# Three gates' units, their PSUM banks and four token sums placed differently in a two-block transformer kernel

## Chip, cores and metric

The kernel runs on one core of one Trainium2 chip (trn2). The metric is the time of one execution on the device in microseconds (us); lower is better. All data are float32. The engines are named as in the profile: PE is TensorE's matmul side and PEld its weight load, DVE is VectorE, ACT is ScalarE, POOL is GpSimd, and SP issues most of the transfers.

## The reference, cut to what matters

256 tokens of width 1024 go through two blocks one after the other. The first block is a token mixer (stick-breaking heads and dilated heads), a norm, 16 experts with two chosen for each token, and a norm. The second block is a mixer (retention of 4 heads beside a latent attention of 8 heads, each with a gate) and then 32 experts with four chosen for each token. The change lies in the two mixers.

```python
def merge_branches(ret_o, ret_gate, att_o, g_ret, g_mla, w_branch_ret, w_branch_mla, w_out):
    r = head_rms(ret_o).reshape(B, L, N_RET_HEADS * RET_V_DIM) * jax.nn.silu(ret_gate)
    m = att_o.reshape(B, L, N_MLA_HEADS * MLA_V_DIM)
    merged = jax.nn.sigmoid(g_ret) * (r @ w_branch_ret) + jax.nn.sigmoid(g_mla) * (m @ w_branch_mla)
    return merged @ w_out
...
    zl = split_proj(h_lat @ w_in)          # rq, rk, rv, rg, cq, ckv, kr, gr, gm
    ql, kl, vl = retention_qkv(zl[0], zl[1], zl[2], rope_fn)
```

## The kernel before

**Weights and phases.** SP streams weights in units of 2 MB into slots of a ring in SBUF, in the order of lists written out by hand: units of phase "a" (first mixer), the 16 experts, units of phase "b" (second mixer), the 32 experts. A unit is loaded as soon as the unit that held its slot has been multiplied, so TensorE's progress sets when transfers start. The number of bytes is the same in both kernels.

**PSUM banks.** There are eight banks. `open_tile` gives a tile the next bank in turn (of 8, or of the first 4 in the first mixer, `among=4`), or a named one, and TensorE waits until the tile that held the bank before has been read out and freed. TensorE executes its list in order, so a wait for one bank holds everything behind it.

**Seven products.** In the second mixer, 14 products of the 256 tokens with 1024 x 512 weights (the list `FAST`) are made by Strassen's scheme with seven products instead of eight, in `seven(i)`, and take three banks each (upper, Z, lower). VectorE makes four differences of each unit's weights (`sum_weights`, L2741) and combines the results (`combine(i)`, L2751 to L2762). ScalarE copies the first product aside (`first_copy(i)`, L2005). The left operands need four sums of the tokens' quarters: `sum_tokens` on VectorE (L2723 to L2726) makes them from the latent tokens once, and, for the unit `rv` of each retention head, from that head's turned tokens `uT`. A gate unit (`rg`: SiLU, `gr`: sigmoid) is read out by ScalarE in `gate_out(i)`, a unit `rq` is rotated by VectorE in `rope` (L2708 to L2714), 2 tiles of 512 columns each.

**Order on TensorE in the second mixer.** It runs seven(0), seven(1) (the two `rq` units), turns the latent tokens back into rows ("hl", L1225), turns the rotated keys and queries (`transposes("rkT", ...)`, `transposes("rqT", ...)`, L522), and runs seven(2). Then comes `scores(0)`, and for each head h of four: a gate's seven(2h+3), the head's turned tokens u (64 matmuls, L1319, with weights that VectorE makes in `weights(h)` from decays that ScalarE makes in `ret_decay(h)`), scores(h+1), and the values' seven(2h+4). Each tile of u is copied to `uT` by ScalarE (signal `uT_ready`). The values' products run in the order 1, 4, 2, 6, 5, 3, 7, and of these 6, 5, 3 and 7 wait for the token sums. A gate's run in the order 1, 6, 5, 2, 3, 7, 4.

**Banks there.** The turn stands at 14 when seven(0) starts, so seven(0) holds banks 6, 7, 0, seven(1) banks 1, 2, 3, the four "hl" tiles 4 to 7, and the four rkT tiles 0 to 3. The upper and lower tile of seven(1) are `rq` rows in banks 1 and 3, which VectorE frees after it has rotated them.

**Order in the first mixer.** TensorE multiplies the dilated values' first tile (`v_dl`, 0), the first two logits, the context's latent (`ckc`, two tiles) and the second tile (`v_dl`, 1). Then it goes through the dilated heads: for head h it turns the softmax's rows (`dl_turn`, L823), multiplies the values of head h-1, and does one other piece (a turn of conditioning rows `ada_turn`, L682, the turn of the context's latent, L760, the next logits). VectorE makes each head's maxima in `dl_max(h)` (L2310 to L2314), ScalarE the exponentials. Before dl_max(2) VectorE scales the stick-breaking heads (`head_norm`, L2326), reads out both ckc tiles and then copies (`v_dl`, 1).

**GpSimd** makes inverse roots on request (`root_of`, L1644), each a small power operation, and issues a few transfers.

## Time and profile before

| | |
|---|---|
| Time, median of 3 runs | 2136.42 us (2136.24 to 2136.6) |
| The profiled execution: own time | 2138.09 us |
| The profiled execution: span from first to last instruction | 2136.3 us |
| TensorE busy | 2059.3 us (96%) |
| VectorE busy | 658.2 us (31%) |
| ScalarE busy | 322.4 us (15%) |
| GpSimd busy | 45.3 us (2%) |
| Mean granted clock of TensorE | 0.992 |
| First mixer | about 10 to 205 us |
| 16 experts | about 205 to 669 us |
| Second mixer | about 669 to 1193 us |
| 32 experts | about 1193 to 2136 us |

The stages are read from the lines of the matmuls in TensorE's timeline. Busy time of a matmul group includes time in which the array runs at the lower clock, so it has to be read together with the granted clock of the stretch.

### The profile page before, as it was taken

Reading aid. Unit: us, or ns where it says so; the run is one execution under the profiler, and the core shown is the slowest. Engines: PE = TensorE matmul, PEld = TensorE weight load, DVE = VectorE, ACT = ScalarE, POOL = GpSimd, SP = SyncE. Lnnn points to the kernel's source line nnn. Section 1 sums busy time; section 2 is a strip of 40 time slices with the busy share of each in tenths; the row PEclk is TensorE's granted clock in tenths of the full one; section 3 lists DMA queues with packets and bytes.
Section 4 is the critical chain, followed back from the end, with each engine's and each line's share of the span. In section 5 each row is a group of like instructions: output and inputs, shape, how many; then the busy total and the mean of one; then the engine's idle time right before and its main releaser. Section 6 shows DMA issues by size and latency. Waiting matters only on the chain.

```text
span 2136.3 us, 23037 instructions
## 1 busy us (share of the span) xinstructions
PE 2059.3 (96%) x9259; PEld 968.1 (45%) x9262; DVE 658.2 (31%) x1286; ACT 322.4 (15%) x505; POOL 45.3 (2%) x66
## 2 busy tenths in 40 slices
PE   9999999989999899999999999999999999999997
PEld 6764333323334688887664433333333333333332
DVE  1665111101113844546551421222222212222213
ACT  1531111001002023212041100111111100111000
POOL 2011000000001000000000000000000000000000
PEclk9999999999999999999999999999999999999999
DMA  9975999999997422324525699999999999999996
GB/s 371 371 296 224 389 424 426 426 427 428 429 429 274 158 79 79 118 94 159 208 111 198 259 412 428 428 428 429 428 429 429 428 428 429 428 428 429 429 427 282
DMA packets 85904, 720.85 MB, mean 337 GB/s; under 512 B 6700, under 2 KB 12065, under 8 KB 46001
## 3 DMA queue, kind: packets, MB, share of 16 engines
q1 hardware_dynamic: 83744, 714.81, 81.0%
q0 software_dynamic: 2096, 5.16, 0.8%
q8 instruction: 44, 0.72, 0.2%
q14 instruction: 20, 0.16, 0.0%
HBM read 718.87 MB, written 1.08 MB: 337 GB/s over the span
## 4 chain that ended last, share of the span: by engine, by line
PE 70%; DMA 23%; DVE 5%; issue 1%; ACT 1%; POOL 0%; DVEq 0%; ACTq 0%; SPq 0%
PE bank L937 17%; PE bank L947 14%; DMA ring<-in_exp_w_gu 10%; DMA ring<-in_w_up 8%; PE bank L1285 6%; DMA pool<-in_exp_w_gu 5%; PE bank L575 4%; PE bank L545 3%; PE bank L954 3%; PE bank L917 3%; PE bank L640 3%; PE bank L1319 3%; PE bank L1376 2%; PE bank L929 2%; DVE ring L2741 1%
## 5 line engine op out<-in xcount | busy, mean ns | idle before, releaser
L937 PE MATMUL bank<-ring,pool 128*64 128x512 f32 x2176 | 485.5, 596 | 18.9 <-DMA ring<-in_w_up 14.9
L947 PE MATMUL bank<-ring,pool 128*64 128x512 f32 x1536 | 341.9, 595 | 9.6 <-DMA ring<-in_exp_w_gu 9.5
L937 PEld LDWEIGHTS bank<-ring,pool 128*64 128x64 f32 x2176 | 149.0, 137 | 310.1 <-issue 275.7
L947 PEld LDWEIGHTS bank<-ring,pool 128*64 128x64 f32 x1536 | 106.2, 137 | 220.0 <-issue 192.2
L1285 PE MATMUL bank<-ring,pool 128*128 128x256 f32 x784 | 172.2, 380 | 3.5 <-ACT ring L2005 1.9
L1285 PEld LDWEIGHTS bank<-ring,pool 128*128 128x128 f32 x784 | 148.5, 190 | 26.5 <-ACT ring L2005 3.1
L2605 DVE TENSOR_SCALAR pool<-bank 128x512 f32<-128x512 f32 x32 | 22.1, 691 | 408.7 <-PE bank L947 408.7
L1925 ACT ACTIVATE pool<-pool 128x512 f32<-128x512 f32 x32 | 20.1, 630 | 733.6 <-DVE pool L2605 733.6
L947 PE MATMUL bank<-pool 128*64 128x512 f32 x512 | 115.6, 594 | 6.4 <-DMA pool<-in_exp_w_gu 6.4
L1745 ACT ACTIVATE pool<-bank 128x512 f32<-128x512 f32 (+2 forms) x112 | 64.2, 573 | 272.9 <-PE bank L594 57.1
L2741 DVE TENSOR_TENSOR ring<-ring 128x1024 f32<-128x1024 f32 x72 | 88.2, 1225 | 34.5 <-issue 16.5
L954 PE MATMUL bank<-pool,junk 64*128 64x512 f32 x392 | 97.4, 615 | 1.5 <-DVE pool L2617 0.8
L917 PE MATMUL bank<-pool 128*64 128x512 f32 x384 | 94.6, 614 | 1.6 <-ACT pool L1745 1.6
L2602 DVE TENSOR_TENSOR pool<-pool,bank 128x512 f32<-128x512 f32 x16 | 17.0, 1059 | 230.1 <-PE bank L937 183.1
L937 PE MATMUL bank<-pool 128*64 128x512 f32 x384 | 86.6, 593 | 0.0
L575 PE MATMUL bank<-ring,pool 128*128 128x512 f32 x192 | 84.3, 594 | 1.4 <-ACTq L1748 1.4
L2617 DVE TENSOR_TENSOR pool<-bank,pool 128x512 f32<-128x512 f32 x32 | 22.1, 691 | 203.6 <-PE bank L937 203.6
L1915 ACT ACTIVATE pool<-bank 128x512 f32<-128x512 f32 x46 | 49.1, 1067 | 182.5 <-PE bank L917 182.5
L545 PE MATMUL bank<-ring,pool 128*128 128x512 f32 (+2 forms) x192 | 75.1, 549 | 1.3 <-DVEq L2296 1.3
L947 PEld LDWEIGHTS bank<-pool 128*64 128x64 f32 x512 | 36.1, 137 | 80.9 <-issue 69.2
L929 PE MATMUL bank<-pool,junk 32*64 32x512 f32 x256 | 61.8, 600 | 0.0
L1644 POOL TENSOR_TENSOR root<-root,power 128x1 f32<-128x1 f32 (+2 forms) x20 | 20.0, 999 | 1860.5 <-DVE root L2996 936.6
(436 smaller groups left out, 1813.9 us busy)
## 6 DMA issues: line engine op xcount, KB each, us to landing
ring<-in_exp_w_gu SPq DMA_DIRECT2D x96, 2048.0 KB, 25.4
ring<-in_exp_w_down SPq DMA_DIRECT2D x46, 2048.0 KB, 28.5
pool<-in_exp_w_gu SPq DMA_DIRECT2D x32, 2048.0 KB, 23.9
ring<-in_w_gate SPq DMA_DIRECT2D x30, 2048.0 KB, 23.1
ring<-in_w_up SPq DMA_DIRECT2D x30, 2048.0 KB, 25.0
ring<-in_w_down SPq DMA_DIRECT2D x30, 2048.0 KB, 21.9
ring<-in_w_in SPq DMA_DIRECT2D x21, 2048.0 KB, 8.2
pool<-in_exp_w_down SPq DMA_DIRECT2D x18, 2048.0 KB, 27.4
```

The costliest lines, as they stand in the source:

```text
L545: i = mm(ps[:, 0:width], src[:, k, t * P:(t + 1) * P], w[:, k, 0:width], start=(k == 0), stop=(k == w.shape[1] - 1))
L575: i = mm(banks[tiles[name, t, f][0]][:, :], srcT[:, kk, t * P:(t + 1) * P], w[:, k, f * 512:(f + 1) * 512], start=(kk == 0), stop=(kk == K ...
L640: i = mm(ps[:, m * T:(m + 1) * T], w[:, k, (2 * mp_ + m) * P:(2 * mp_ + m + 1) * P], xT[:, k, :], start=(k == 0), stop=(k == KC - 1))
L917: i = mm(XG[half[f], :], pick[:, t, :], src[:, t, f * 512:(f + 1) * 512], start=(t == 0), stop=(t == TC - 1))
L929: i = mm(dst[half[f], :], this_expert, bgu_rows[:, at:at + 512], start=True, stop=False)
L937: i = mm(dst[half[f], :], chunks[kk], rows[k][:, f * 512:(f + 1) * 512], start=(kk == 0), stop=(kk == KC - 1))
L947: i = mm(dst[half[f], :], chunks[2 * j + k], wide[:, k, at:at + 512], start=False, stop=(j == 3 and k == 1))
L954: i = mm(Y[t, f][:, :], put[half[f], t * P:(t + 1) * P], y_slot[half[f], :], start=False, stop=last, skip_group_check=True)
L1285: ins = mm(dst, left[:, k, :], right[:, k, :], start=(k == 0 and p != 2), stop=(k == 3), skip_group_check=True)
L1319: i = mm(ps[:, c * T:(c + 1) * T], in_rows[:, j, k * P:(k + 1) * P], dec2[:, j, :], start=(j == 0), stop=(j == 3))
L1745: freed(af(dst, view(ps), func, scale=scale), name)
L2741: mark(tt(to, x, y, ALU.subtract), "w_summed")
```

## The change

Five things change.

1. In `FAST`, the unit ("rg", 2) moves ahead of ("rv", 0). TensorE now runs seven(2) (the unit ("rg", 0)) between "hl" and the turns of keys and queries, with banks 2, 6, 7, and seven(3) after these turns, with banks 5, 6, 7. The turns get named banks: rkT 3, 4, 5, 6 and rqT 0, 1, 3, 4. The turn is rounded up to a multiple of 8 before seven(0) and before scores(0). Head 0's filler is seven(4) (("rg", 2)), head 1 has none, head 2's is seven(7), head 3's seven(9). The values' sevens are 5, 6, 8 and 10.
2. ScalarE reads out in the matching order: the four rkT tiles, gate_out(2), the four rqT tiles, first_copy(3), ret_decay(0), gate_out(3), first_copy(4). `first_copy(i)` also waits for the combined upper tile of i-1.
3. The four sums of each head's turned tokens are made by GpSimd, which waits for `uT_ready`, and for its own first sum, before it goes on. VectorE no longer makes them.
4. In the first mixer (`v_dl`, 0) goes to bank 4 and takes no turn of the four, the two ckc tiles swap banks 4 and 6, (`v_dl`, 1) is copied out by ScalarE instead of VectorE, and the context's latent is read out by VectorE behind dl_max(3) and turned by TensorE in head 3 instead of head 2.
5. Ahead of the first experts' placement, TensorE runs three warming matmuls (bf16, 512 columns) where it ran none.

```diff
-        FAST = (("rq", 0), ("rq", 1), ("rg", 0), ("rg", 1), ("rv", 0), ("rg", 2), ("rv", 1), ("rg", 3), ("rv", 2), ("gr", 0), ("rv", 3), ("gr", 1),
+        FAST = (("rq", 0), ("rq", 1), ("rg", 0), ("rg", 1), ("rg", 2), ("rv", 0), ("rv", 1), ("rg", 3), ("rv", 2), ("gr", 0), ("rv", 3), ("gr", 1),
                 ("gm", 0), ("gm", 1))
+        FILLER = {h: FAST.index(x) for h, x in ((0, ("rg", 2)), (2, ("rg", 3)), (3, ("gr", 0)))}
+        VALUE = [FAST.index(("rv", h)) for h in range(RH)]
...
-                ps = open_tile(pe, ("ckc", t), bank=(4, 6)[t])
+                ps = open_tile(pe, ("ckc", t), bank=(6, 4)[t])
...
-            by_rows([("v_dl", 0)], "a", n, part("a", n, KC, 512), [(xT, 0)], 512, among=4, last=False)
+            by_rows([("v_dl", 0)], "a", n, part("a", n, KC, 512), [(xT, 0)], 512, bank=4, last=False)
...
-                if h == 2:
+                if h == 3:
                     turn_context_latent()
...
-                keep_warm(ps, 0 if m == "m1" else 3)
+                keep_warm(ps, 3)
...
+            turn[0] += -turn[0] % 8
             for u in range(2):
                 seven(u)
             turn_back("hl", latT)
+            seven(2, (2, 6, 7))
             pe.wait_ge(S("rotated"), 4)
-            transposes("rkT", rk_rows, 4)
+            transposes("rkT", rk_rows, 4, at=(3, 4, 5, 6))
             pe.wait_ge(S("rotated"), 8)
-            transposes("rqT", rq_rows, 4)
-            seven(2)
+            transposes("rqT", rq_rows, 4, at=(0, 1, 3, 4))
+            seven(3, (5, 6, 7))
+            turn[0] += -turn[0] % 8
...
             for h in range(RH):
-                seven(2 * h + 3)
+                if h != 1:
+                    seven(FILLER[h])
...
-                seven(2 * h + 4)
+                seven(VALUE[h])
             seven(11)
...
-            inverse_roots(*([TC] * (RH + 2)))
+            for h in range(RH):
+                (x11, x12), (x21, x22) = token_quarters(uT)
+                s1, s2, s3, s4 = (u_sums[:, q] for q in range(4))
+                pool_eng.wait_ge(S("uT_ready"), 4 * h + 4)
+                if h > 0:
+                    pool_eng.wait_ge(S("product"), 7 * VALUE[h - 1] + 7)
+                nc.gpsimd.tensor_tensor(s1, x21, x22, ALU.add).then_inc(S("root_set"), 1)
+                pool_eng.wait_ge(S("root_set"), 2 * h + 6)
+                nc.gpsimd.tensor_tensor(s2, s1, x11, ALU.subtract).then_inc(S("root_set"), 1)
+                nc.gpsimd.tensor_tensor(s3, x11, x21, ALU.subtract)
+                pool_eng.wait_ge(S("root_set"), 2 * h + 7)
+                nc.gpsimd.tensor_tensor(s4, x12, s2, ALU.subtract).then_inc(S("tokens_summed"), 1)
+                inverse_roots(TC)
+            inverse_roots(TC, TC)
...
+                if h == 1:
+                    evac(v_dl[:, 1, :], ("v_dl", 1), lambda ps: ps[:, :], "v_ready")
...
             first_copy(2)
+            for cp in range(4):
+                evac(pairs(rkT[1], cp), ("rkT", cp), two, "rkT_ready", RQK ** -0.5)
+            gate_out(2)
+            for cp in range(4):
+                evac(pairs(rqT, cp), ("rqT", cp), two, "rows_and_rqT")
+            first_copy(3)
             ret_decay(0)
-            gate_out(2)
-            first_copy(3)
+            gate_out(3)
+            first_copy(4)
...
-            take_root(ckc_ss, 2 * HEADS, ckc_root)
-            for t in range(TC):
-                ps = tile(dve, ("ckc", t))
-                link(v.tensor_copy(krc[:, t, :], ps[:, KVR:CKR]))
-                mark(ts(ckn_c[:, t, :], ps[:, 0:KVR], ckc_ss[:, t:t + 1], None, ALU.mult), "ckc_ready")
-                freed(dve.nop(), ("ckc", t))
-            values_out("v_dl", v_dl, (1,))
+            def context_latent_out():
+                take_root(ckc_ss, 2 * HEADS, ckc_root)
+                for t in range(TC):
+                    ps = tile(dve, ("ckc", t))
...
 
             for h in range(2, HEADS):
                 dl_max(h)
+                if h == 3:
+                    context_latent_out()
...
             combine(2)
+            combine(3)
             weights(0)
             for h in range(RH):
-                combine(2 * h + 3)
-                dve.wait_ge(S("uT_ready"), 4 * h + 4)
-                sum_tokens(2 * h + 4)
+                if h != 1:
+                    combine(FILLER[h])
                 if h + 1 < RH:
                     weights(h + 1)
-                combine(2 * h + 4)
+                combine(VALUE[h])
```

## Rows read from the trace of the kernel before

**Rows 1.** The profile's page: busy time of the engines, and the chain that ended last
```profile
PE 2059.3 (96%) x9259; PEld 968.1 (45%) x9262; DVE 658.2 (31%) x1286; ACT 322.4 (15%) x505; POOL 45.3 (2%) x66
...
PE 70%; DMA 23%; DVE 5%; issue 1%; ACT 1%; POOL 0%; DVEq 0%; ACTq 0%; SPq 0%
```

**Rows 2.** What TensorE waited for: us in total, times, longest
```profile
PE bank L522 <- DVEq L2771: 7.3, 2, 6.0
...
PE bank L682 <- DVEq L2200: 2.9, 1, 2.9
```

**Rows 3.** TensorE's timeline: start, us, line, operation [idle before it, ended by]
```profile
739.51 1.91 PE L1225 MATMUL bank<-cst,pool 128*128 128x128 f32 x16
741.26 0.60 PE L522 MATMUL bank<-cst,ring 128*128 128x128 f32 x4
747.86 1.97 PE L522 MATMUL bank<-cst,ring 128*128 128x128 f32 x8 [6.00 <-DVEq L2771]
...
754.87 1.46 PE L1285 MATMUL bank<-ring,pool 128*128 128x256 f32 x6
```

**Rows 4.** Stretches: busy us of each engine, granted clock, DMA share, GB/s
```profile
137.00:143.00 6.00, 6.00 (x31) 5.27 (x30) 3.11 (x12) 3.20 (x11) 0.00 (x0) 0.50 1.01 414
744.00:755.00 11.00, 5.88 (x29) 5.48 (x30) 6.21 (x15) 3.32 (x6) 0.00 (x0) 0.53 0.26 100
...
1203.00:1204.00 1.00, 0.64 (x5) 0.58 (x6) 0.76 (x5) 0.00 (x0) 0.00 (x0) 1.00 0.00 0
```

**Rows 5.** TensorE's timeline, retention head 0
```profile
799.76 13.98 PE L1285 MATMUL bank<-ring,pool 128*128 128x256 f32 x64
814.02 3.72 PE L1285 MATMUL bank<-ring,pool 128*128 128x256 f32 x16 [0.28 <-DVE ring L2741]
818.37 7.17 PE L1285 MATMUL bank<-ring,pool 128*128 128x256 f32 x32 [0.62 <-ACT ring L2005]
```

**Rows 6.** TensorE's timeline, retention head 3
```profile
925.87 24.44 PE L1285 MATMUL bank<-ring,pool 128*128 128x256 f32 x112 [0.73 <-ACTq L1748]
```

**Rows 7.** VectorE's timeline, second mixer
```profile
736.74 0.42 DVE L2751 TENSOR_TENSOR ring<-ring,bank 128x256 f32<-128x256 f32 x1 [0.35 <-DVEq L2772]
...
743.01 0.42 DVE L2762 TENSOR_TENSOR bank<-bank,ring 128x256 f32<-128x256 f32 x1
...
750.55 0.42 DVE L2714 TENSOR_TENSOR pool<-pool 128x256 f32<-128x256 f32 x1
...
797.26 0.69 DVE L2723 TENSOR_TENSOR pool<-pool 128x512 f32<-128x512 f32 x1 [11.97 <-ACTq L1748]
...
807.17 0.69 DVE L2787 TENSOR_TENSOR pool<-pool 128x512 f32<-128x512 f32 x1 [7.16 <-ACT pool L1993]
```

**Rows 8.** ScalarE's timeline, second mixer
```profile
740.15 2.74 ACT L1745 ACTIVATE ring<-bank 128x512 f32<-128x512 f32 x4 [10.35 <-PE bank L1225]
...
757.20 1.28 ACT L1990 ACT_TABLE_LOAD   x1
```

**Rows 9.** GpSimd's timeline
```profile
186.24 0.55 POOL L1644 TENSOR_TENSOR root<-root,power 128x1 f32<-128x1 f32 x1 [19.20 <-DVE root L2173]
188.29 2.35 POOL L1696 TENSOR_TENSOR pool<-pool 128x1024 f32<-128x1024 f32 x1 [1.50 <-DVE pool L2433]
...
1173.15 0.53 POOL L1634 DMA_DIRECT2D pool<-in_exp_b_down  x1 [0.29 <-POOL pool L1718]
```

**Rows 10.** TensorE's timeline, first mixer
```profile
135.76 0.63 PE L682 MATMUL bank<-cst,misc 128*128 128x128 f32 x4 [2.92 <-DVEq L2200]
...
146.87 0.55 PE L823 MATMUL bank<-cst,pool 128*128 128x128 f32 x3
```

**Rows 11.** VectorE's timeline, first mixer
```profile
131.44 1.42 DVE L2326 TENSOR_TENSOR pool<-pool,stat 128x512 f32<-128x512 f32 x2
...
135.80 0.42 DVE L2310 TENSOR_TENSOR pool<-bank,pool 128x256 f32<-128x256 f32 x1 [0.24 <-DVE pool L2199]
...
138.38 0.16 DVE L2251 TENSOR_TENSOR mod<-bank,vecT 128x16 f32<-128x16 f32 x1
```

More of the change, by code:

```diff
@@ L537, in by_columns, with by_rows @@
                     multiplied(phase, n, (name, 1))
-            def by_rows(names, phase, n, w, srcs, width, among=8, last=True):
+            def by_rows(names, phase, n, w, srcs, width, among=8, last=True, bank=None):
                 landed(phase, n)
                 for name, (src, t) in zip(names, srcs):
-                    ps = open_tile(pe, name, among=among)
+                    ps = open_tile(pe, name, among=among, bank=bank)
                     for k in range(w.shape[1]):
@@ L1260, in _, with seven @@
             rk_rows_of(0, 1)
-            def seven(i):
+            def seven(i, at=(None, None, None)):
                 (first, second), sums = token_quarters(tokens_of(i)[0]), tokens_of(i)[1]
@@ L1267, in seven @@
                 landed("b", n)
-                Xb = open_tile(pe, upper)
-                Zb = open_tile(pe, ("seven", i))
-                Yb = open_tile(pe, lower)
+                Xb, Zb, Yb = (open_tile(pe, name, bank=b) for name, b in zip((upper, ("seven", i), lower), at))
                 sources = 2 + FAST[i][1] if FAST[i][0] == "rv" else 1
@@ L1718, in _ @@
             nc.gpsimd.memset(y_slot, 0.0).then_inc(S("root_set"), 1)
-            pool_eng.wait_ge(S("root_set"), 6)
+            pool_eng.wait_ge(S("root_set"), 14)
             for f in range(2):
@@ L2002, in first_copy @@
             def first_copy(i):
+                if i > 0:
+                    tile(act, row_tiles(i - 1)[0])
                 act.wait_ge(*after_product(i, 1))
@@ L2018, in _ @@
             first_copy(0)
-            tile(act, ("rq", 0, 0))
             first_copy(1)
             rows_back("hl", 2)
-            for cp in range(4):
-                evac(pairs(rkT[1], cp), ("rkT", cp), two, "rkT_ready", RQK ** -0.5)
-            for cp in range(4):
-                evac(pairs(rqT, cp), ("rqT", cp), two, "rows_and_rqT")
             def gate_out(i):
@@ L2035, in _ @@
             first_copy(2)
+            for cp in range(4):
[4 more added lines that the diff above has]
+            first_copy(3)
             ret_decay(0)
-            gate_out(2)
-            first_copy(3)
+            gate_out(3)
+            first_copy(4)
             rss = stat[:, 36:44]
             for h in range(RH):
-                gate_out(2 * h + 3)
+                if h != 1:
+                    gate_out(FILLER[h])
                 for g in range(4):
                     evac(pairs(uT, g), ("u", h, g), two, "uT_ready")
-                first_copy(2 * h + 4)
+                first_copy(VALUE[h])
                 if h + 1 < RH:
@@ L2050, in _ @@
                     act.wait_ge(S("ret_ss"), 2 * h + t + 1)
-                first_copy(2 * h + 5)
+                if h > 0:
+                    first_copy(VALUE[h] + 1)
             gate_out(11)
@@ L2065, in _ @@
             first_copy(12)
-            tile(act, ("gm", 0, 0))
             first_copy(13)
@@ L2362, in _ @@
             head_norm(0, "y_sb_ready")
-            take_root(ckc_ss, 2 * HEADS, ckc_root)
-            for t in range(TC):
-                ps = tile(dve, ("ckc", t))
-                link(v.tensor_copy(krc[:, t, :], ps[:, KVR:CKR]))
-                mark(ts(ckn_c[:, t, :], ps[:, 0:KVR], ckc_ss[:, t:t + 1], None, ALU.mult), "ckc_ready")
-                freed(dve.nop(), ("ckc", t))
-            values_out("v_dl", v_dl, (1,))
+            def context_latent_out():
+                take_root(ckc_ss, 2 * HEADS, ckc_root)
+                for t in range(TC):
+                    ps = tile(dve, ("ckc", t))
+                    link(v.tensor_copy(krc[:, t, :], ps[:, KVR:CKR]))
+                    mark(ts(ckn_c[:, t, :], ps[:, 0:KVR], ckc_ss[:, t:t + 1], None, ALU.mult), "ckc_ready")
+                    freed(dve.nop(), ("ckc", t))
             for h in range(2, HEADS):
                 dl_max(h)
+                if h == 3:
+                    context_latent_out()
                 if h == 3:
@@ L2794, in _ @@
             combine(2)
+            combine(3)
             weights(0)
             for h in range(RH):
-                combine(2 * h + 3)
-                dve.wait_ge(S("uT_ready"), 4 * h + 4)
-                sum_tokens(2 * h + 4)
+                if h != 1:
+                    combine(FILLER[h])
                 if h + 1 < RH:
                     weights(h + 1)
-                combine(2 * h + 4)
+                combine(VALUE[h])
                 dve.wait_ge(S("ret_ss"), 2 * h + 2)
```

## The prediction

> **What bounds the kernel now.** I read the page first: TensorE is busy 96% of the span, and 70% of the chain that ended last lies on it, 23% on transfers [rows 1]. So only time in which TensorE stands still, or runs at the lower of its two clock levels, can be won. Two stages differ in kind. The experts end transfer-bound: SP can't hand over weights faster than they come, and their stretch has its full length from the moment its stream starts. Is a saving ahead of them kept? The stretches say yes: just before the second stream starts the transfer engines are idle (share 0.00 from 1203 to 1204 [rows 4]), since they wait for slots that TensorE frees. Whatever moves TensorE's list in the mixers forward moves the streams too.
>
> The view of TensorE's waits then names the two large ones that aren't transfers: 7.3 us in two waits for VectorE ahead of the transposes of L522, and 2.9 us ahead of the conditioning rows' turn, L682 [rows 2]. The timelines place them. In the second mixer TensorE finishes the "hl" turns at 741.26, turns one tile of keys and stands still for 6.0 us; its next full product starts at 754.87 [rows 3]. VectorE rotates the last `rq` rows until 750.97 (750.55 + 0.42) [rows 7], and these rows hold banks 1 and 3 that the turned keys want. The granted clock is 0.53 on average from 744 to 755 [rows 4]: it is the lower level, 1.2 GHz, nearly throughout, and it was the upper level before TensorE stopped. In the first mixer it is the same on a small scale: a wait of 2.92 us [rows 10], then 0.50 from 137 to 143 [rows 4].
>
> **The keys' and queries' turns.** From 741.26 to 754.87 pass 13.6 us for 32 transposes. Sixteen such took 1.75 us at the upper level (739.51 to 741.26 [rows 3]), so the work is 3.5 us and 10.1 us are standstill and clock. Now seven(2) stands there. It wants banks 2, 6, 7; 6 and 7 hold the first "hl" tiles, which ScalarE copies from 740.15 at 0.69 us each (2.74 for four [rows 8]), so the second is free at 741.5: 0.3 us of waiting. Two sevens took 24.44 us [rows 6], so one is 12.1 net of overlap and it ends at 753.65. By then the rotation is over and its banks 3 and 5 are free; 32 transposes run to 757.15.
>
> **The new wait.** seven(3) wants bank 7, which holds the lower tile of seven(2). VectorE's combine(2) starts behind the rotation at 751.3 and needs 6.7 us (736.74 to 743.43 [rows 7]), so that tile is combined at 758.0. ScalarE has four key tiles ahead of it (754.3 to 757.1), then a table load of 1.28 us for the SiLU [rows 8], then two tiles at 0.69: bank 7 is free at 759.75. TensorE waits 2.6 us (1.5 at best, if ScalarE isn't the last; 3.5 if its copies queue). The waits ahead of a drop of the clock were 6.0 and 2.92 us, both behind short transposes and small matmuls; 2.6 us behind transposes is near the second, so I take a drop as likelier than not. It can cost from nothing to 3.0 us (6.0 us at half speed in rows 4); the wait is the shorter one, and I take 1.7. Sum of this part: 10.1 - 0.3 - 2.6 - 1.7 = 5.5 us won (3 to 8.3).
>
> **The pairs.** When two sevens follow each other TensorE waits 0.28 us for the second's weight differences and 0.62 us for ScalarE's first copy, because VectorE came late out of `weights(h+1)` [rows 5]. The trace has this three times, in heads 0, 1 and 2. Now head 0's values are followed by head 1's u matmuls, which want none of this, so one pair goes: 0.9 us won. What these matmuls want is `weights(1)`: 807.17 plus four operations of 0.7 us, so 810.0 [rows 7], 10.2 us after the start of the head's seven, which lasts 12.1. It holds with 1.9 us to spare.
>
> **The sums on GpSimd.** VectorE's sums aren't on the path: it had stood idle for 11.97 us before them and waits 7.16 us for ScalarE's decays behind them [rows 7]. So taking them off wins nothing. Putting them on GpSimd costs nothing only if they are in time. The first three products of a values' seven (24 matmuls, 5.2 us by rows 6) want no sums. In heads 0 to 2 `scores` lies between as well: sums from 797.26, matmuls from 799.76 [rows 5, 7], so GpSimd has 7.7 us. In head 3 the seven starts as soon as ScalarE's last copy is out [rows 6], and it has 5.2. The trace has one two-input operation on GpSimd, 2.35 us for 1024 columns [rows 9]. For 512 the bounds are half of it, 1.18, and, if nothing shrinks, 2.35. With a fixed part as large as its smallest power operation, 0.55 [rows 9], it is 1.45; I take 1.3. Four and one wait on itself, 0.29 [rows 9], make 5.5 us: in time by 2 us in three heads, late by 0.4 in the last. At 2.35 it would be 9.7 us: late by 2.0 three times and by 4.5 once, 10.5 us. At 1.18 it is in time everywhere.
>
> A rule speaks against this part. The Trainium skill (GPSIMD Engine Reference, "Engine selection") gives elementwise work to VectorE, as GpSimd is about twice as slow with two inputs. The trace agrees roughly: 2.35 us against VectorE's 0.69 for half the columns. The same page measured 4497 ns for 2048 columns; an estimate by proportion is 1.12 us for 512, by which head 3 would not be late and the sum would be 0.4 us better.
>
> **The first mixer.** (`v_dl`, 1) holds the bank that the conditioning rows' turn takes, and VectorE copied it behind the ckc tiles. ScalarE now copies it at once. VectorE comes to head 2's maxima at 132.86 instead of 135.80 [rows 11], so the wait of 2.92 us shrinks to some 0.6, until head 2's logits are read. The two ckc tiles (2.0 us: 2.94 less the `v_dl` copy and its wait) are now behind dl_max(3), ahead of conditioning(1), which comes 2.6 us after dl_max(2) starts (135.80 to 138.38 [rows 11]). So it comes at 132.86 + 2.6 + 2.0 = 137.5, and head 2's turn wants its bank at 135.9: a new wait of 1.8. Before, 2.92 of standstill and 3.0 of clock; now 0.6 and 1.8, and a drop at 1.7. Won: 5.9 - 4.1 = 1.8 us (0.4 if the clock costs what it did, 3.5 if it stays up), as an earlier turn of head 4 than 146.87 [rows 10].
>
> **The rest.** The three warming matmuls lie where TensorE waits for VectorE's choice; I count 0 (up to 1.2 won in the clock). The rg unit's earlier load moves no bytes. SP waits for products only, and the next unit lands in the twelve microseconds of a seven. The other banks of the second mixer shift by two for all tiles alike behind the heads, so nothing else meets. One more ScalarE table load lies ahead of head 0, where ScalarE waits anyway.
>
> **Sum.** 5.5 + 0.9 - 0.4 + 1.8 = 7.8 us. The profiled execution's span of 2136.3 becomes 2128.5; its own time, 2138.09, is 1.7 above the median of the runs, so I subtract from the median: 2136.4 - 7.8 = 2128.6 us.
>
> **Rivals.** (a) The clock stays up in both places: 3.4 us more, and with the warming and the short bank wait up to 13 won: about 2125 to 2123. For it: the new waits are shorter than both that dropped it. Against: they follow small work. (b) The waits only move: bank 7 at 3.5 us, drops at their full 3.0 in both places, GpSimd a microsecond late: 7.8 - 0.9 - 2.6 - 1.0 leaves 3.3 us won, about 2133. For it: both moved readings queue behind ScalarE or VectorE. (c) GpSimd is late in every head, because an operation on these strided quarters costs as much as on 1024 columns: 7.8 + 0.4 - 10.5 loses 2.3 us, about 2138.7. The sign turns at 2.2 us an operation. Against it: then VectorE's idle stretch would be the only reason to move them, and the one operation seen has no large fixed part. (d) The saving isn't kept because the experts' streams don't move: no change, 2136. Against it: the idle transfer engines at 1203.
>
> **How the numbers follow.** This kernel's measurement tells about 0.2% (4.3 us) from no change. Forecast (5 to 10 us won) 0.60, (a) 0.13, (b) 0.16, (c) 0.07, (d) 0.04. Faster by over 0.2%: the forecast, (a) and a third of (b), 0.78. Within: the rest of (b), (d) and most of (c), 0.18. Slower: 0.04. The range reaches into (a) and (b): 2124 to 2133.
>
> **What the profile after would show.** In the turns' place a wait of TensorE on ScalarE (bank 7) of 1.5 to 3.5 us and a granted clock near 0.5 for a short stretch behind it; seven(2) directly behind "hl"; two pairs of 0.28 and 0.62 instead of three; GpSimd operations of 1.2 to 1.45 us and, in head 3 alone, a wait of TensorE on GpSimd of about 0.4; in the first mixer two waits below 2 us. It goes wrong if GpSimd takes over 1.9 us an operation, if bank 7 comes over 4 us late, or if TensorE waits for `weights(1)`.

## The result, and the profile after

The changed kernel takes 2123.4 us (median of 5 runs, 2122.52 to 2127.22), the kernel before 2136.6 us (5 runs, 2136.24 to 2138.15): ratio 0.9939, 95% interval 0.9925 to 0.9952. That is 13.2 us won where 7.8 were forecast, 0.6 us under the low end of the range. The profiled execution of the changed kernel took 2122.52 us, its span is 2120.7 us against 2136.3: 15.6 us less. That is 2.4 us more than the medians differ by: the changed kernel's profiled execution was the fastest of its five, and the one before (2138.09 us) was above its median. Its mean granted clock is 0.996 against 0.992. Most line numbers shift: the sevens are still L1285, the turns of keys and queries L524, the "hl" turn L1227, u L1323, the conditioning rows' turn L684, the softmax's L825, the first copy L2026, the decays L2009 to L2012.

What TensorE waited for in the changed kernel (us in total, times, longest); these two answer to [rows 2]:

```profile
PE bank L1285 <- ACT ring L1762: 2.8, 2, 2.6
...
PE bank L825 <- DVEq L2276: 2.0, 1, 2.0
```

The 7.3 us for VectorE ahead of the keys' turns are gone, and the 2.9 us ahead of the conditioning rows as well. A wait of 2.6 us for ScalarE has come in the one place and one of 2.0 us for VectorE in the other. TensorE's timeline from "hl" to head 0's second product, against [rows 3]:

```profile
734.79 1.91 PE L1227 MATMUL bank<-cst,pool 128*128 128x128 f32 x16
736.88 12.33 PE L1285 MATMUL bank<-ring,pool 128*128 128x256 f32 x56 [0.18 <-ACT ring L1762]
749.05 1.91 PE L524 MATMUL bank<-cst,ring 128*128 128x128 f32 x16
750.79 1.91 PE L524 MATMUL bank<-cst,pool 128*128 128x128 f32 x16
755.28 14.01 PE L1285 MATMUL bank<-ring,pool 128*128 128x256 f32 x56 [2.57 <-ACT ring L1762]
...
772.58 2.75 PE L1285 MATMUL bank<-ring,pool 128*128 128x256 f32 x12
```

seven(2) follows "hl" after 0.18 us, both turns take 1.91 us each (the upper clock level), and then seven(3) waits 2.57 us for bank 7. ScalarE's timeline in that place shows what it waited for:

```profile
749.68 2.74 ACT L1762 ACTIVATE pool<-bank 128x512 f32<-128x512 f32 x4 [10.35 <-PE bank L524]
752.53 1.28 ACT L1762 ACT_TABLE_LOAD   x1
753.82 1.31 ACT L1762 ACTIVATE ring<-bank 128x512 f32<-128x512 f32 x2
755.25 2.74 ACT L1762 ACTIVATE pool<-bank 128x512 f32<-128x512 f32 x4
```

It is the forecast's queue: four key tiles, the table load of 1.28 us, the two SiLU tiles, the last out at 755.13; TensorE goes on at 755.28. The stretches (busy us of each engine, granted clock, DMA share, GB/s), against [rows 4]:

```profile
744.00:755.00 11.00, 8.70 (x57) 7.79 (x55) 9.42 (x17) 4.73 (x7) 0.00 (x0) 1.00 0.43 150
755.00:761.00 6.00, 5.72 (x19) 4.79 (x20) 0.00 (x0) 5.31 (x10) 0.00 (x0) 0.72 0.21 77
137.00:143.00 6.00, 4.01 (x40) 3.56 (x40) 4.95 (x17) 2.65 (x9) 0.00 (x0) 1.00 1.00 417
...
196.00:200.00 4.00, 4.00 (x10) 1.93 (x10) 3.13 (x16) 0.23 (x1) 0.00 (x0) 0.57 0.76 236
```

744 to 755 ran at 1.00 where it had 0.53. Behind the new wait the clock fell (0.72 over these six microseconds), and seven(3) takes 14.01 us where seven(2) took 12.33: 1.7 us. The same work, seven(0) to seven(3), "hl", the turns and scores(0), took 67.16 us before (715.34 to 782.50) and takes 61.96 (710.62 to 772.58): 5.2 won. In the first mixer 137 to 143 has 1.00 where it had 0.50.

The heads, against [rows 5]; TensorE's timeline of heads 1 and 2:

```profile
831.29 24.42 PE L1285 MATMUL bank<-ring,pool 128*128 128x256 f32 x112
855.54 13.98 PE L1323 MATMUL bank<-pool,ring 128*128 128x256 f32 x64
...
872.81 13.98 PE L1285 MATMUL bank<-ring,pool 128*128 128x256 f32 x64
887.13 3.72 PE L1285 MATMUL bank<-ring,pool 128*128 128x256 f32 x16 [0.35 <-DVE ring L2767]
891.48 7.17 PE L1285 MATMUL bank<-ring,pool 128*128 128x256 f32 x32 [0.63 <-ACT ring L2026]
898.50 13.98 PE L1323 MATMUL bank<-pool,ring 128*128 128x256 f32 x64
```

Head 2's pair still has its waits, 0.35 and 0.63. Head 1's runs through, 112 matmuls without one. From the start of the pair to the next u it is 24.25 us in head 1 and 25.69 in head 2, and it was 25.62 in each of heads 0 to 2 before (799.76 in [rows 5] to 825.38, where head 1's u starts). In head 0 the two sevens now stand apart and take 12.09 each (772.58 to 784.67), 24.18 together. So two pairs went, at 1.4 us each.

Why head 1's has no wait is in ScalarE's timeline of the changed kernel, head 1:

```profile
833.28 0.38 ACT L2026 ACTIVATE ring<-bank 128x256 f32<-128x256 f32 x1 [4.65 <-PE bank L1285]
833.56 0.59 ACT L2009 ACTIVATE pool<-cst,lg 128x256 f32<-128x256 f32 x1
```

The decays start 0.28 us after the first copy starts. In the kernel before, in the same head, a table load lies between:

```profile
844.58 0.38 ACT L2005 ACTIVATE ring<-bank 128x256 f32<-128x256 f32 x1 [4.58 <-PE bank L1285]
844.98 1.28 ACT L1990 ACT_TABLE_LOAD   x1
846.27 0.60 ACT L1990 ACTIVATE pool<-cst,lg 128x256 f32<-128x256 f32 x1
```

There a SiLU had been done since the last exponential. Head 1 has no gate now, so the exponential's table is still there.

GpSimd's timeline in head 3, the tightest, against [rows 9]:

```profile
913.23 1.26 POOL L1717 TENSOR_TENSOR pool<-pool 128x512 f32<-128x512 f32 x1 [20.69 <-ACTq L1765]
...
917.03 1.26 POOL L1722 TENSOR_TENSOR pool<-pool 128x512 f32<-128x512 f32 x1
```

These are the first and the last of four; 1.26 us each, 5.06 from start to end (913.23 to 918.29), and no row of TensorE's waits names these lines. The first mixer, against [rows 10]:

```profile
135.19 0.52 PE L825 MATMUL bank<-cst,pool 128*128 128x128 f32 x3 [0.44 <-DVEq L2336]
...
139.29 0.52 PE L825 MATMUL bank<-cst,pool 128*128 128x128 f32 x3 [1.99 <-DVEq L2276]
...
140.27 1.04 PE L524 MATMUL bank<-cst,pool 128*128 128x128 f32 x8
```

Two waits, 0.44 and 1.99, where there was one of 2.92; the eight transposes behind take 1.04 us, the upper level.

**By stage.** Stages are cut at the first matmul of the first mixer's output product (L577), the first long experts' product (L939), seven(0), and the matmuls behind the last seven of the heads (L547). us in each stage, in profiled executions:

| kernel | start to L577 | to L939 | to seven(0) | second mixer to L547 | to the end |
|---|---|---|---|---|---|
| before | 159.16 | 60.05 | 496.13 | 234.80 | 1186.2 |
| changed | 156.88 | 57.89 | 495.85 | 226.88 | 1183.2 |
| difference | -2.28 | -2.16 | -0.28 | -7.92 | -3.0 |

Only the first and fourth column hold edited work. The second and the last lose 5.2 us though nothing that lies there but the three warming matmuls was touched. Before, the profiled execution ran at the lower level within five stretches (136 to 144, 194 to 198, 208 to 212, 744 to 755, 1198 to 1202), about 27 us; the changed kernel's within three (106 to 112, 196 to 200, 756 to 760), about 10 us. Some six microseconds at the very end, at the lower level in both, are left out of these sums. The experts keep what the mixers win: their stage, L939 to seven(0), is 494.4 to 496.2 us long in the profiled executions of all kernels here, and the last transfer-bound product moves from 2109.02 to 2093.80.

### The profile page after: what moved, and what is told of

Read it like the earlier page. It is cut to its first block, busy times and chain, and to the rows that moved or that the text cites. A ratio compares the mean times of both kernels' runs of the same rounds, so it can differ in the third digit from the quotient of the medians.

```text
span 2120.7 us, 23046 instructions
## 1 busy us (share of the span) xinstructions
PE 2053.0 (97%) x9262; PEld 963.5 (45%) x9265; DVE 647.0 (31%) x1269; ACT 321.5 (15%) x505; POOL 65.3 (3%) x82
## 4 chain that ended last, share of the span: by engine, by line
PE 72%; DMA 23%; DVE 3%; ACT 1%; issue 1%; POOL 0%; DVEq 0%; ACTq 0%; SPq 0%
PE bank L939 17%; PE bank L949 14%; DMA ring<-in_exp_w_gu 10%; DMA ring<-in_w_up 8%; PE bank L1285 8%; DMA pool<-in_exp_w_gu 5%; PE bank L577 4%; PE bank L547 3%; PE bank L956 3%; PE bank L642 3%; PE bank L1323 3%; PE bank L919 3%; PE bank L1380 2%; PE bank L931 2%; PE bank L965 1%; PE bank L924 1%
## 5 line engine op out<-in xcount | busy, mean ns | idle before, releaser
L939 PE MATMUL bank<-ring,pool 128*64 128x512 f32 x2176 | 485.6, 596 | 18.4 <-DMA ring<-in_w_up 14.6
L939 PEld LDWEIGHTS bank<-ring,pool 128*64 128x64 f32 x2176 | 148.9, 137 | 310.0 <-issue 275.5
L1285 PE MATMUL bank<-ring,pool 128*128 128x256 f32 x784 | 173.3, 382 | 4.5 <-ACT ring L1762 2.8
L1285 PEld LDWEIGHTS bank<-ring,pool 128*128 128x128 f32 x784 | 149.6, 191 | 27.4 <-issue 3.8
L939 PE MATMUL bank<-pool 128*64 128x512 f32 x384 | 86.6, 593 | 0.0
L577 PE MATMUL bank<-ring,pool 128*128 128x512 f32 x192 | 84.3, 594 | 1.5 <-ACTq L1765 1.4
L547 PE MATMUL bank<-ring,pool 128*128 128x512 f32 (+2 forms) x192 | 76.8, 559 | 1.3 <-DVEq L2320 1.3
```

The source lines that it names most:

```text
L547: i = mm(ps[:, 0:width], src[:, k, t * P:(t + 1) * P], w[:, k, 0:width], start=(k == 0), stop=(k == w.shape[1] - 1))
L577: i = mm(banks[tiles[name, t, f][0]][:, :], srcT[:, kk, t * P:(t + 1) * P], w[:, k, f * 512:(f + 1) * 512], start=(kk == 0), stop=(kk == K ...
L939: i = mm(dst[half[f], :], chunks[kk], rows[k][:, f * 512:(f + 1) * 512], start=(kk == 0), stop=(kk == KC - 1))
L1285: ins = mm(dst, left[:, k, :], right[:, k, :], start=(k == 0 and p != 2), stop=(k == 3), skip_group_check=True)
```

## Experiments

Twelve kernels, in three groups of four, each group timed on one chip with the kernel before beside it: 2137.03 us for the first four, 2137.35 for the next four, 2136.80 for the last four. Ratios and gains are against the kernel before of the same group.

**Second mixer alone.** The changed kernel with the first mixer, the warming and the sums as before:

```diff
-            by_rows([("v_dl", 0)], ..., 512, bank=4, last=False)
+            by_rows([("v_dl", 0)], ..., 512, among=4, last=False)
...
-                keep_warm(ps, 3)
+                keep_warm(ps, 0 if m == "m1" else 3)
...
+                dve.wait_ge(S("uT_ready"), 4 * h + 4)
+                sum_tokens(VALUE[h])
```

> The kernel before with the second mixer's new order and banks alone; the four token sums stay on VectorE, the first mixer and the warming are as before. If the order does it: 5.2 us from the turns of keys and queries and 2.7 us from two pairs of sevens that no longer wait, so about 7.9 us under before (a slow clock level more or less moves it by 1.7). Rival: the sums on GpSimd are what ended head 1's pair of waits, because they took work off VectorE; then only head 0's pair goes here and the gain is 6.5 us, and the pair of sevens in head 1 still takes 25.6 us to the next head's u instead of 24.2.

Measured: 2127.44 us, ratio 0.9955 (0.9939 to 0.9972), 9.6 us won. TensorE's timeline:

```profile
759.22 12.32 PE L1285 MATMUL bank<-ring,pool 128*128 128x256 f32 x56 [2.58 <-ACT ring L1749]
```

The same wait, 2.58, but the seven behind it takes 12.32: here the clock did not fall. The stage from seven(0) to L547 is 225.20 us, 9.6 less than before's 234.80, which is also the difference of the medians. That is 1.7 us more than expected, and at the upper clock level, as the expectation allowed. Head 1's pair has no wait here either, with the sums still on VectorE.

**First mixer alone.** The kernel before with the fourth edit of the change only:

```diff
-            by_rows([("v_dl", 0)], ..., 512, among=4, last=False)
+            by_rows([("v_dl", 0)], ..., 512, bank=4, last=False)
...
-            values_out("v_dl", v_dl, (1,))
...
+                if h == 3:
+                    context_latent_out()
```

> The kernel before with the change in the first mixer alone (banks, the copy of the values on ScalarE, the context's latent read out one head later). If the clock's level is the larger part: 3.7 us under before, with no stretch at the lower level between 130 and 145 us and one wait of 2.0 us for the conditioning rows' bank. Rival: the clock drops behind that wait in this surrounding, and the gain is 1.8 us.

Measured: 2135.17 us, ratio 0.9988 (0.9978 to 0.9997), 1.9 us won by the medians; the interval holds 0.6 to 4.7. Its trace has the two waits, 0.44 and 1.99, and the clock falls at 138 to 142 (0.57 over these four microseconds), so the rival's 1.8 us is what came.

**Warming alone.** The kernel before with three warming matmuls ahead of the first experts' placement.

> The kernel before with the three warming matmuls ahead of the first experts' placement alone. If they hold the clock up through the first gather, it ends 1.1 us earlier and the kernel is 1 to 2 us under before. Rival: the missing drop there came from the other parts' shift in time, and this run is at before within 1 us, with the gather of eight matmuls at 3.1 us as before.

Measured: 2136.82 us, ratio 0.9999 (0.9989 to 1.0009). Nothing.

**GpSimd's sums alone.** The kernel before with the third edit only.

> The kernel before with the four sums of each head's turned tokens on GpSimd alone. If they are in time and VectorE was idle there: within 1 us of before, no wait of TensorE on GpSimd. Rival: they help VectorE, or their reading slows it: 1 us or more under or over before.

Measured: 2137.02 us, ratio 1.0002 (0.9992 to 1.0011). No wait on GpSimd in the trace.

**The changed kernel with the sums on VectorE.**

> The changed kernel with the four token sums of each head back on VectorE, all else as changed. If GpSimd's part is neutral: the same time as the changed kernel, about 13 us under before within 1.5, and head 1's two sevens still without a wait. Rival: VectorE's 2.8 us of sums in head 1 come ahead of the weights and bring that pair's wait back; then 1.4 us slower than the changed kernel.

Measured: 2126.15 us, ratio 0.9947 (0.9933 to 0.996), an interval that overlaps the changed kernel's. The gain, 11.2 us, is a little under what was expected; the median is 2.8 us above the changed kernel's first and 1.2 above its second measurement (below), within its runs (2122.52 to 2127.22). TensorE's timeline in head 1:

```profile
832.36 24.43 PE L1285 MATMUL bank<-ring,pool 128*128 128x256 f32 x112
856.62 13.98 PE L1323 MATMUL bank<-pool,ring 128*128 128x256 f32 x64
```

The pair takes 24.26 us without a wait, and the stage from seven(0) to L547 is 225.21 us, as with the second mixer alone. So it is not the sums that took the waits away, and they cost this stage nothing on either engine.

**The table load put back.** The changed kernel, with a SiLU of one column on ScalarE in head 1, whose result nothing reads:

```diff
                     evac(pairs(uT, g), ("u", h, g), two, "uT_ready")
+                if h == 1:
+                    act.wait_ge(S("first_copied"), VALUE[0] + 1)
+                    link(af(junk[:, 0:1], stat[:, 0:1], ACT.Silu))
                 first_copy(VALUE[h])
```

> The changed kernel with one SiLU of a single column added on ScalarE in head 1 ahead of the copy of the values' first product, so that its exponential table has to be loaded again for the next head's decays, as in the kernel before. If the table load is why head 1's pair no longer waits: TensorE's waits of 0.3 and 0.6 us return in head 1, and from its values' seven to the next head's u it takes 25.6 us instead of 24.25; 1.4 us slower than the changed kernel. Rival: something else (GpSimd's sums) ended it, and the pair stays at 24.25.

Measured: 2126.19 us, ratio 0.9945 (0.993 to 0.996). TensorE's and ScalarE's timelines in head 1:

```profile
834.72 13.98 PE L1285 MATMUL bank<-ring,pool 128*128 128x256 f32 x64
849.07 3.72 PE L1285 MATMUL bank<-ring,pool 128*128 128x256 f32 x16 [0.38 <-DVE ring L2770]
853.42 7.17 PE L1285 MATMUL bank<-ring,pool 128*128 128x256 f32 x32 [0.63 <-ACT ring L2026]
860.43 4.91 PE L1323 MATMUL bank<-pool,ring 128*128 128x256 f32 x22
```

```profile
837.13 1.28 ACT L2009 ACT_TABLE_LOAD   x1
838.43 0.60 ACT L2009 ACTIVATE pool<-cst,lg 128x256 f32<-128x256 f32 x1
```

The load is back between the first copy and the decays, and with it both waits: 834.72 to 860.43 is 25.71 us, as in head 2, and the stage from seven(0) to L547 is 228.37 us, 1.5 more than the 226.9 of the other two executions in which the clock fell behind the 2.57 us wait, as it did here. The SiLU itself and the load for it run from 832.16 to 833.66, with ScalarE idle for the 3.07 us between them and the first copy, so they hold nothing up; what is new behind the first copy is the second load alone, and it is the cause. The 0.38 and 0.63 make 1.01 of the 1.45 us that this pair is longer than 24.26. The rest is in the breaks: the three groups are busy 13.98 + 3.72 + 7.17 = 24.87 us, and one unbroken group 24.42, so each break adds 0.22 us. In these records matmuls overlap: one alone takes 0.38 us on average, and the unbroken 112 start every 0.22 us. A break forgoes an overlap. Since the profile models the ends of matmuls, the split of the 1.45 us is less sure than the 1.45 us.

**GpSimd's chain made longer.** The changed kernel, with the first of the four sums made five times over:

```diff
-                nc.gpsimd.tensor_tensor(s1, x21, x22, ALU.add).then_inc(S("root_set"), 1)
-                pool_eng.wait_ge(S("root_set"), 2 * h + 6)
+                for r in range(5):
+                    nc.gpsimd.tensor_tensor(s1, x21, x22, ALU.add).then_inc(S("root_set"), 1)
+                    pool_eng.wait_ge(S("root_set"), 6 * h + 6 + r)
```

> The changed kernel with GpSimd's first sum made five times with a wait between, so its chain takes eight operations and some 10.5 us instead of 5.1. If the deadline was read rightly (7.7 us in heads 0 to 2, 5.2 us in head 3): TensorE waits 2.8 us in each of heads 0 to 2 and 5.3 us in head 3, 13.7 us more than the changed kernel without a drop of the clock, up to 7 more with drops. If the products want the sums later than I read, less than 10 us.

Measured: 2141.49 us, ratio 1.0028 (1.0018 to 1.0038). TensorE's waits for GpSimd, and GpSimd's and TensorE's timelines in head 0:

```profile
PE bank L1285 <- POOL pool L1723: 13.7, 4, 5.1
```

```profile
796.76 6.63 POOL L1718 TENSOR_TENSOR pool<-pool 128x512 f32<-128x512 f32 x5 [115.42 <-ACTq L1766]
...
805.92 1.26 POOL L1723 TENSOR_TENSOR pool<-pool 128x512 f32<-128x512 f32 x1
```

```profile
807.33 7.97 PE L1285 MATMUL bank<-ring,pool 128*128 128x256 f32 x28 [2.69 <-POOL pool L1723]
...
932.07 21.71 PE L1285 MATMUL bank<-ring,pool 128*128 128x256 f32 x88 [5.13 <-POOL pool L1723]
```

The chain is 10.42 us (796.76 to 807.18) and TensorE waits 2.69, so the sums are wanted 7.7 us after they can start; in head 3 (932.07) it waits 5.13, which puts the deadline at 5.3. The real chain of 5.06 has 2.7 us to spare in head 0 and 0.2 in head 3. The waits are 13.7 us in all, and the clock fell behind three of them.

**The changed kernel without the warming.**

> The changed kernel without the three warming matmuls ahead of the first experts. If they carry part of the gain: 1 to 2 us slower than the changed kernel, with the first gather at 3.1 us again. If the missing drop was the profiled execution's own: within 1 us of the changed kernel.

Measured: 2122.64 us, ratio 0.9929 (0.9914 to 0.9944), the changed kernel's time. With the warming alone at 0.9999, no effect of that edit is seen in either setting.

**The first mixer's queue on VectorE turned round.** The changed kernel, with conditioning(1) ahead of the context's tiles:

```diff
-                if h == 3:
-                    context_latent_out()
                 if h == 3:
                     conditioning(1)
+                    context_latent_out()
```

> VectorE copies the turned conditioning rows in front of the context's latent tiles in the last step of the first mixer's loop; all else as in the changed kernel. Theory (the 1.99 us wait of the changed kernel is the queue on VectorE: the two ckc tiles lie ahead of the conditioning rows): the wait goes or stays under 0.6 us, the first output matmul of the first mixer starts 1.5 to 2 us earlier than at 156.88, and the time is 1.5 to 2 us under the changed kernel's, about 2121.5 us. Rival (the ckc copies are then late for what follows them, the projection of the context's keys): as long a wait of TensorE appears one product later, and the time stays.

Measured: 2122.45 us, ratio 0.9938 (0.9924 to 0.9951). TensorE's timeline:

```profile
137.49 0.52 PE L825 MATMUL bank<-cst,pool 128*128 128x128 f32 x3
...
140.22 0.66 PE L524 MATMUL bank<-cst,pool 128*128 128x128 f32 x4 [1.16 <-DVEq L2336]
...
141.60 0.52 PE L825 MATMUL bank<-cst,pool 128*128 128x128 f32 x3 [0.29 <-DVEq L2336]
...
156.93 1.52 PE L577 MATMUL bank<-ring,pool 128*128 128x512 f32 x3
```

The wait of 1.99 is gone: head 2's turn stands at 137.49 without one. But the transposes of L524 behind it wait 1.16 us and head 3's turn 0.29, both released by VectorE, and the output product starts at 156.93 where it did at 156.88 (from the ckc tiles on that is 39.52 us against 39.65). So the expectation was right on the queue and wrong on the gain, and the rival, that the wait moves to what follows, holds. The median is 1.0 us under the changed kernel's first measurement and 2.5 under its second, on the same chip (below); the intervals overlap, and the stage that was edited shows no such gain.

**A free bank for the second key unit's product.** The changed kernel, with seven(3) in banks 5, 6, 0, and ScalarE reading the query tiles and the first copy before the gate:

```diff
-            seven(3, (5, 6, 7))
+            seven(3, (5, 6, 0))
...
-            scores(0)
+            scores(0, (1, 2))
+            turn[0] += 5
...
+                if h == 0:
+                    seven(FILLER[h], (3, 4, 7))
...
-            gate_out(2)
             for cp in range(4):
                 evac(pairs(rqT, cp), ("rqT", cp), two, "rows_and_rqT")
             first_copy(3)
+            gate_out(2)
```

> The second key unit's product takes bank 0 instead of bank 7 for its third tile, ScalarE reads out the key tiles' turns and this product first and does the gate and head 0's decays behind; head 0's scores and the product behind them take other banks accordingly. Theory (the 2.57 us wait is for bank 7, which waits for ScalarE's SiLU with its table load): the wait falls to 0.3 to 0.9 us, the clock doesn't drop in 756 to 760, and the time is 1.9 us (wait alone) to 3.7 us (wait and clock) under the changed kernel's. Rival (ScalarE's later gate and decays hold up head 0's weights): a new wait of TensorE of 1 to 3 us at head 0's output matmuls and a time equal to the changed kernel's within 1 us.

Measured: 2118.86 us (2117.22 to 2122.39), ratio 0.9919 (0.9906 to 0.9933). TensorE's timeline:

```profile
754.93 12.32 PE L1285 MATMUL bank<-ring,pool 128*128 128x256 f32 x56 [0.58 <-ACT pool L1765]
...
782.63 13.98 PE L1326 MATMUL bank<-pool,ring 128*128 128x256 f32 x64
```

The wait is 0.58 us, now for the first query tile, which holds bank 0 and is read out behind the four key tiles; the clock stays up, and nothing new waits at head 0's u. The stage from seven(0) to L547 takes 223.22 us, 2.0 less than the 225.2 of executions with the 2.57 us wait at full clock. By the medians it is 4.5 us under the changed kernel's first measurement and 6.1 under the one below. The traces show 2.0 of it, and 1.7 more against executions where the clock had fallen behind the wait; the rest isn't accounted for.

**Both of these edits.**

> Both of the two edits above together. Theory: they lie in different stages and add, 3.5 to 5.5 us under the changed kernel's, about 2118 to 2120 us. Rival: the clock's drops move to other places as before, so that less than 3 us is seen, 2121 or more.

Measured: 2119.15 us (2118.76 to 2120.22), ratio 0.992 (0.9907 to 0.9934): the time of the bank's edit alone, as the first mixer's gave nothing. Against the kernel with the first mixer's edit, 2122.45 us on the same chip, the bank's edit wins 3.3 us here, where it won 4.5 and 6.1 above; the stage from seven(0) to L547 is 223.21 us, again 2.0 less.

**The changed kernel once more,** unedited, on the chip of the last three.

> The changed kernel itself, unedited, on the same chip as the three above, so that they can be set against it. Theory (the clock's drops behind waits of 1.3 to 2.6 us differ from execution to execution, the waits don't): the waits of 0.44, 1.99 and 2.57 us are there again within 0.2 us, the stretches at the lower clock are not all the same, and the time is 2122 to 2127 us. Rival (the drops belong to the program): the same stretches as in the first profile of it.

Measured: 2124.94 us (2122.59 to 2126.54), ratio 0.9946 (0.9932 to 0.9959). TensorE's timeline, and two stretches:

```profile
757.04 12.32 PE L1285 MATMUL bank<-ring,pool 128*128 128x256 f32 x56 [2.60 <-ACT ring L1762]
```

```profile
137.00:143.00 6.00, 5.37 (x34) 5.09 (x38) 4.53 (x14) 1.55 (x4) 0.00 (x0) 0.72 1.01 414
...
755.00:761.00 6.00, 3.96 (x18) 3.53 (x19) 1.27 (x2) 5.17 (x9) 0.00 (x0) 1.00 0.52 198
1184.00:1190.00 6.00, 5.10 (x19) 1.49 (x19) 2.07 (x10) 0.00 (x0) 0.00 (x0) 0.72 0.80 339
```

The waits are the same, 1.99 and 2.60. The lower clock isn't: here 137 to 143 has 0.72, 755 to 761 has 1.00, and 1184 to 1190 has 0.72 (1.00, 0.72 and 1.00 in the first profile of the same instructions).

**The drops over all profiled executions.** Each of the four with the 6.0 us wait (before and the three with the old second mixer) ran about 10 us at the lower level, from within the wait on. Each of the four with the 2.92 us wait in the first mixer (before, the second mixer alone, the warming alone, the sums alone) had a drop behind it: the granted clock is 0.50 over six microseconds in before and 0.72 in the other three. Of the eight with the 2.57 us wait three did (the changed kernel's first profile, the one with the table load, the one without warming); of the eight with the 1.99 us wait in the first mixer six did. Of all fourteen, eight had one behind the wait of 1.30 us that lies ahead of (`v_dl`, 0) in every kernel here (107.62 in the changed kernel's first profile, 107.84 in before's, which had none).

## Why the prediction was right in kind and short in size

| term | predicted | in the changed kernel's profiled execution |
|---|---|---|
| turns of keys and queries | 5.5 | 5.2; 6.9 in executions where the clock stays up |
| pairs | 0.9 | 2.7 (two at 1.4, less 0.1 in head 2) |
| GpSimd's sums | -0.4 | 0 |
| first mixer | 1.8 | 3.8 from (`v_dl`, 1) on (the waits 0.7 shorter together, with one of 0.23 that the kernel before has at 136.62; the clock 3.0) |
| not in the sum: ahead of (`v_dl`, 1) | 0 | -1.5 (a drop at 106 to 112, 1.7) |
| not in the sum: the stages without edits | 0 | 5.4 |
| sum | 7.8 | 15.6 |

**The turns: right.** The waits were forecast at 0.3 and 2.6 us and are 0.18 and 2.57, with the forecast's queue on ScalarE as cause. The drop behind it, taken as likelier than not at 1.7 us, cost 1.7 where it came, but it came in three of eight, so the forecast's reason for it, that 2.6 us is near 2.92, isn't borne out.

**The pairs: the term that failed.** "So one pair goes: 0.9 us won." Two went, at 1.4 us. A pair was priced by its two idle times, and not by the overlap lost at each break (twice 0.22 us); the whole price could be had from [rows 5] and [rows 6], as 25.78 us from the broken pair's start to its end (799.76 to 818.37 + 7.17) against 24.44 for the unbroken one, 1.3 us. And head 1's ScalarE was not followed: the price came from `weights(h+1)` being late, whose lateness was ScalarE's table load behind a SiLU, and head 1 lost its gate. [rows 8] had the load's 1.28 us; the prediction counted one load more ahead of head 0 and missed the one less in head 1. Together 1.8 us. This is the step that failed for certain, and it isn't enough by itself: with 2.7 in place of 0.9 the sum is 9.6 us, and the forecast 2126.8, still within the range. The other 3.4 us are in the last paragraph of this section, and in part stay open.

**GpSimd: right, a little dear.** An operation took 1.26 us (forecast 1.3, bounds 1.18 and 2.35), the chain 5.06 (5.5), and the wait of 0.4 us in head 3 didn't come. The deadlines of 7.7 and 5.2 us are measured at 7.7 and 5.3. Rival (c) needed 2.2 us. Neither engine's sums are on the path: the two kernels that moved them alone show 1.0002 and a time inside the changed kernel's spread. The rule of the Trainium skill (GPSIMD Engine Reference, "Engine selection"), that VectorE is to have elementwise work, holds as to speed, 1.26 us against VectorE's 0.69, and decides nothing here. The estimate from the Trainium skill's figure on the same page, 1.12 us, was low by 0.14.

**The first mixer: waits right, clock not.** 0.6 and 1.8 us were forecast, 0.44 and 1.99 came. The drop was charged 1.7 us and didn't come in this execution, but came in six of eight. Alone, the edit gave 1.9 us by the medians, the forecast's size. The 3.8 us of the profiled executions are mostly luck of the clock: from (`v_dl`, 1) to L577 before took 34.68 us with the clock at 0.50 over six microseconds, but 33.1 to 33.5 in the three other executions with the old order, at 0.72; with the new order it is 33.9 to 34.0 in two at about 0.5, 32.5 to 32.6 in four at 0.72, and 30.9 in the two without a drop. At like clock the edit is worth some 0.7 us. The 3.0 us that the forecast charged the old order for its clock were read from the dearest of four executions.

**Warming, `weights(1)`, the streams: right.** The warming shows nothing in either direction; u of head 1 starts at 814.02 without a wait; the saving reaches the end, so rival (d) is out.

**What made the time fall out of the range.** In the second mixer, whose stage took 225.2 to 225.3 us in all four executions with the change's order, its sums in time and no drop (226.9 in two with one), 6.0 us were forecast (5.5 + 0.9 - 0.4) and 9.6 came in the executions without a drop: 1.8 for the pairs, 0.4 for GpSimd, 1.7 minus 0.3 for the turns. With the first mixer's 1.9 that is 11.5 us, and the changed kernel's two measurements won 13.2 and 11.9. So the mechanism was the forecast's, with the clock at (a)'s end more often than the forecast allowed; the range's low end of 2124 left no room for a mis-sized term on top of it. What is over 11.5 us lies, as far as the profiled executions tell, in the stages without edits, where drops come and go: from L577 to L939 took 57.8 to 57.9 us in eight profiled executions and 59.2 to 60.4 in six, with either order of the first mixer in both groups. The last stage, from L547 on, took 1183.2 to 1184.1 us in the six executions without a drop between 1184 and 1202, the changed kernel's first among them, and 1185.5 to 1186.8 in the eight with one, before's among them; so its 3.0 us are mostly one such drop. Whether the shorter waits make those drops rarer on the whole (the mean clock of single runs is 0.991 to 0.994 for the kernel before and 0.995 to 0.997 in the changed kernel's ten) or only their own places' is not settled; no kernel here changed the clock without changing the work.

## What to carry to other kernels

Price a stall by the start-to-start length of the work around it, broken against unbroken, and not by its idle time alone. When a reorder takes an operation out of a loop's step, follow its engine through that step: a table load can go or come with it, and what it held back stands in another engine's queue. When a moved wait is for one bank, look which banks are free at that moment before accepting it: naming bank 0 instead of 7, with ScalarE's readings put in the matching order, won 2.0 us of its stage at like clock (3.3 to 6.1 by the medians, in part not accounted for), where three of this change's five edits (the first mixer's, the sums', the warming's) won 1.9, 0 and 0 by themselves.

## What the runs showed of the hardware

- A two-input operation on GpSimd took 1.26 us for 128x512 and 2.36 for 128x1024 in the changed kernel: by a straight line through the two, an estimate, 0.16 us fixed and 2.15 ns a column.
- The same instruction list ran at the lower clock in different stretches from one execution to the next, also where TensorE was 4.00 us busy of 4 (196 to 200). Behind waits of 1.30, 1.99 and 2.57 us the drop was neither sure nor absent (8 of 14, 6 of 8, 3 of 8); behind those of 2.92 and 6.0 us it came in all four executions. Where it came behind seven(3)'s wait it cost 1.7 us in each of the three.
- A break in a chain of 128x256 matmuls cost 0.22 us beyond the idle time that the profile shows (1.45 us for two breaks with 1.01 us idle).
- A switch of ScalarE from one function to another cost its load of 1.28 us and little more: from the end of the last key tile's copy (752.42) to the start of the first SiLU (753.82) it is 1.40 us.
